# A decoder layer with mixture of experts on one core: the loop over expert passes, run as blocks of eight passes

## The chip, the cores and the metric

The kernel runs on one core of one Trainium2 chip. The metric is the device time of one execution, in microseconds (us). A core has five engines, each with a sequencer of its own that reads its instructions: PE (matrix products), DVE (vector), ACT (scalar), POOL and SP (here it only issues transfers). Loops, branches, register arithmetic and waits are run by the sequencers, and every engine runs its own copy of each loop.

## The reference

One decoder layer on 512 tokens of width 1024, in float32, and a final RMSNorm. Behind the attention part stands the part that fills most of the time, a mixture of 32 experts of which each token uses 4:

```python
def moe(x2d, w_router, b_router, w_in, b_in, w_out, b_out):
    logits = (x2d @ w_router).astype(jnp.float32) + b_router.astype(jnp.float32)
    top_val, top_idx = lax.top_k(logits, TOP_K)
    gates = jax.nn.softmax(top_val, axis=-1)
    ...
    def expert_block(args):
        xb, e = args
        h = xb @ w_in[e] + b_in[e]
        glu = jnp.minimum(h[:, ::2], SWIGLU_LIMIT)
        lin = jnp.clip(h[:, 1::2], -SWIGLU_LIMIT, SWIGLU_LIMIT)
        act = glu * jax.nn.sigmoid(SWIGLU_ALPHA * glu) * (lin + 1.0)
        return act @ w_out[e] + b_out[e]
    ...
    return jax.ops.segment_sum(y, tok_s, num_segments=N)
```

## The kernel before

**Passes.** The tokens of each expert are served in passes of at most 128 (SLOTS). How many passes there are is known only once the router has run: an expert with up to 128 tokens takes one. The bound is MAX_PASSES = 512 * 4 / 128 + 31 = 47; with these inputs there are 33. DVE works out two small tables, `pass_expert` (the expert of each pass) and `pass_first` (its first slot), by way of `pass_diag` and one matmul, each of MAX_PASSES + 1 columns.

**The loop.** Pass 0 is written out. `by_pass` (L441 to L445) then runs passes 1 and up on each engine: a loop over p from 1 to MAX_PASSES - 1 (L443), in which a test (L444) jumps over the body where p isn't below the number of passes. The loop has no early exit, so it counts on to its end. Behind it, `after_last` (L454) reads the number of the last pass from memory, and the rest of the work is written out.

**A pass.** Its weights come as 12 chunks of 1 MB, loaded by SP (`load`, L481) into a ring of 6 slots; a slot is free when ACT and DVE have both read its last chunk. ACT rounds each chunk (`make_hi`, L1084) and DVE takes the rest (`make_lo`, L1514), so that PE can form float32 products from three passes over the chunk (L839, L841, L847). A chunk is 12 matmuls. Four chunks make the first half of the up product of pass p, four the down product of pass p - 1, four the second half of the up product of p. Between them PE makes a list of tokens (L806) and transposes (L814, L865); ACT takes the sigmoid (L1099), DVE makes the rest of SwiGLU (L1526, L1527, L1530); `act_hi` (L1104) and `act_lo` (L1535) split the transposed result. ACT scales the down product's rows (`scale_rows`, L1110). POOL prepares the next list (`prepare_list`, L1706 to L1711), for which DVE's `slots_one_hot` (L1498) waits, gathers the next tokens' rows (L1725) and scatters the result (L1732).

**Behind the loop** comes the down product of the last pass: four chunks, on PE

```python
            done = after_last(pe)
            pe.wait_ge(down_banks_free, done)
            down(done, 0, 0)
            act_transposes(done - 1, 1)
            down(done, 1, 1)
            pe.wait_ge(actT_lo_made, done * 2)
            down(done, 2, 2)
            down(done, 3, 3)
```

SP loads these chunks and then the four parts of the scattered results (parts 0 to 2 at L535, 2 MB each, part 3 in four pieces at L538). The load of part 0 waits until ACT and DVE have read the last chunk of the loop, that of part 1 for two more chunks, that of part 2 for all; part 3 also for the last scatter. DVE's order is: chunks 0 and 1 (`make_lo`), SwiGLU, chunk 2, additions 0 and 1 of part 0 (L1608), `act_lo`, addition 2, chunk 3, addition 3, and then the four additions of each of parts 1, 2 and 3. The final norm and the stores follow.

Of the kernel before, what the change touches and what calls it, by code (L numbers as in the profile page):

```python
# [28 lines left out]
BF16 = mybir.dt.bfloat16  # L29
I32 = mybir.dt.int32  # L30
U32 = mybir.dt.uint32
ALU = mybir.AluOpType
# [17 lines left out]
NE = 32  # L50
# [15 lines left out]
PARTS = 3  # L66
SLOTS = P
MAX_PASSES = SEQ * TOPK // SLOTS + NE - 1
STEPS_PER_PASS = 4
STEPS_TO_ROUTE = 5  # L70
ACT_LIMIT = LIMIT / (1.0 + math.exp(-SWI_ALPHA * LIMIT))
# [11 lines left out]
C_IDENT, C_DECAY, C_QDEC, C_KDEC, C_FREQ = 0, 128, 640, 896, 900  # L83
# [24 lines left out]
def build(nc, x, positions, norm1_g, w_in, lambda_q1, lambda_k1, lambda_q2, lambda_k2, diff_norm_g,  # L108
# [3 lines left out]
    with ctx:  # L112
        def sb(name, shape, dt=F32):
            return ctx.enter_context(nc.sbuf_tensor(name, shape, dt))

        def sem(name):
            return ctx.enter_context(nc.semaphore(name))
# [23 lines left out]
        cst = sb("cst", [P, C_N])  # L141
# [5 lines left out]
        ones_bf = sb("ones_bf", [P, P], BF16)  # L147
# [9 lines left out]
        row_bias = sb("row_bias", [P, 2, 2])  # L157
        row_sum = sb("row_sum", [P, 2, 2])
        row_rec = sb("row_rec", [P, 2, 2])
        pass_expert = sb("pass_expert", [1, MAX_PASSES + 1], I32)  # L160
        passes_upto = sb("passes_upto", [1, NE], I32)
        last_pass = sb("last_pass", [1, 1], I32)
        pos_cur = sb("pos_cur", [P, NT])
# [17 lines left out]
        def w(a, n, rows=P):  # L181
            return work[0:rows, a:a + n]
# [29 lines left out]

        route = w(18944, NT * NE * 4).rearrange("p (i e c) -> p i e c", i=NT, e=NE)
        slot_of = w(19456, NT * NE).rearrange("p (i e) -> p i e", i=NT)
        pass_first = w(19584, MAX_PASSES + 1)
        cum_passes = w(19680, NE)
        n_passes = w(19712, NE)
        expert_count = w(19744, NE)
        scatters_upto = w(19824, NE, 1).bitcast(I32)
        earlier = w(7680, NE)  # L220
        pass_col = w(7712, 4)
        pass_diag = w(7744, MAX_PASSES + 1).bitcast(BF16).rearrange("p (a n) -> p a n", a=2)
        logits = w(20096, NE)
        top8 = w(20128, 8)
        top8_f = w(20136, 8)
# [39 lines left out]
        bank = [pair[i // 2][:, i % 2, :] for i in range(8)]  # L265
# [86 lines left out]
        table_ready = sem("table_ready")  # L352
# [87 lines left out]

        def by_pass(eng, body):  # L441

            with eng.Fori(1, MAX_PASSES) as p:  # L443
                with eng.If(p < passes[eng]):  # L444
                    body(p)  # L445

        passes = {}

        def load_pass_count(eng):
            eng.wait_ge(table_ready, 2)  # L450
            passes[eng] = eng.value_load(at(passes_upto, NE - 1), min_val=1, max_val=MAX_PASSES)

        def after_last(eng):
            return eng.value_load(last_pass[0:1, 0:1], min_val=0, max_val=MAX_PASSES - 1) + 1  # L454

# [92 lines left out]
        def _(pe):  # L548
# [261 lines left out]
            def x_transposes(p, a):  # L810
                if a == 0:
                    pe.wait_ge(gathered, 16 * (p + 1))
                for k in range(KH):
# [4 lines left out]
            gate_transpose(2)  # L818
            gate_transpose(3)
            pe.wait_ge(diag_ready, 1)  # L820
            pe.matmul(bank[7][:, 128:128 + 2 * (MAX_PASSES + 1)], ones_bf[:, :],
                      pass_diag.rearrange("p a n -> p (a n)"), start=True, stop=True).then_inc(pass_rows, 1)
            bias_product(2)
            token_list(0)
# [341 lines left out]
        def _(dve):  # L1166
            chain = Chain(dve, dve_step)
# [295 lines left out]
            for n in range(SLOTS, SEQ, SLOTS):  # L1463
# [16 lines left out]
            chain(dve.tensor_tensor(pass_col[:, 2:3], pass_number, pass_col[:, 1:2], ALU.subtract))  # L1480
            chain.settle()

            near = cst[:, C_IDENT:C_IDENT + MAX_PASSES + 1]
            chain(dve.tensor_scalar(pass_diag[:, 0, :], near, pass_col[:, 0:1], None, ALU.mult))
            dve.tensor_scalar(pass_diag[:, 1, :], near, pass_col[:, 2:3], None, ALU.mult).then_inc(diag_ready, 1)
            dve.wait_ge(pass_rows, 1)
            chain(dve.tensor_scalar(pass_first, bank[7][:, 128 + MAX_PASSES + 1:128 + 2 * (MAX_PASSES + 1)],
                                    float(SLOTS), None, ALU.mult))

            dve.tensor_scalar(pass_expert[:, :], bank[7][0:1, 128:128 + MAX_PASSES + 1], float(NE - 1), None, ALU.min).then_inc(table_ready, 1)  # L1490
            dve.wait_ge(table_ready, 2)
            chain.settle()

# [95 lines left out]
            def counted_pass(p):  # L1589
                chain.before = start + (p - 1) * STEPS_PER_PASS  # L1590
                one_pass(p)
                assert chain.n == STEPS_PER_PASS, chain.n

            by_pass(dve, counted_pass)
            done = after_last(dve)
            chain.before, chain.n = start + (done - 1) * STEPS_PER_PASS, 0
            make_lo(done, 0)
# [24 lines left out]
            chain = Chain(dve, tail_step)  # L1622
# [181 lines left out]
```

## Time and profile before

| what | value |
|---|---|
| time, median of 3 runs | 1616.66 us (1616.61 to 1617.23) |
| span of the profiled execution | 1615.8 us |
| PE busy | 1528.0 us, 95% |
| DVE busy | 1323.2 us, 82% |
| ACT busy | 1007.7 us, 62% |
| POOL busy | 320.3 us, 20% |
| moved by DMA | 476.46 MB |
| span of the loop's passes | about 390 to 1570 us |

The span runs from the first to the last instruction of the one execution that was profiled. It has no other time of its own; the median of the runs is 0.9 us above it. Times in rows are from the span's start. Busy time counts what an engine works, not the register, branch and wait instructions of its sequencer; those appear only where a source line is asked for, under the engine's name with a q (PE's under PEld). The granted clock is given as a share of 2.4 GHz.

### The profile page before, as it was taken

What the parts mean: (1) busy time and instruction counts of PE and PEld (TensorE: products, weight loads), DVE (VectorE), ACT (ScalarE), POOL (GpSimd) and SP (SyncE); (2) the same over time, 40 slices, a digit from 0 to 9 for tenths busy, and PEclk for the clock granted to TensorE, in tenths of its full rate; (3) what the DMA queues carried; (4) which work ended last, traced back from release to release, by engine and by line L of the source; (5) the groups of instructions that cost most, each with busy time, mean ns of one, the idle gap of its engine ahead of it and who ended that gap; (6) DMA issues with size and microseconds to landing.
All of it is one profiled execution on the core that took longest, in us unless ns stands there. A gap on an engine that the chain in (4) does not pass through costs nothing.

```text
span 1615.8 us, 23914 instructions
## 1 busy us (share of the span) xinstructions
PE 1528.0 (95%) x7535; PEld 1253.7 (78%) x7535; DVE 1323.2 (82%) x1276; ACT 1007.7 (62%) x898; POOL 320.3 (20%) x382
## 2 busy tenths in 40 slices
PE   5999679979999999999999999999999999999983
PEld 5999458747888888888888888888888888888872
DVE  3732771368999999998999999999999999999977
ACT  5221551225777777777777777777777777777762
POOL 1000301001222222222222222222222222221210
PEclk9999799859999999999999999999999999999996
DMA  9300701018999999999999999999999999999995
GB/s 266 105 27 1 260 1 46 27 39 294 341 362 366 357 367 364 367 364 368 372 350 361 362 363 369 370 357 376 359 375 347 359 362 366 365 369 363 366 338 222
DMA packets 140909, 476.46 MB, mean 295 GB/s; under 512 B 12160, under 2 KB 28816, under 8 KB 140816
## 3 DMA queue, kind: packets, MB, share of 16 engines
q1 hardware_dynamic: 128096, 445.17, 73.5%
q0 software_dynamic: 10496, 28.74, 5.4%
q10 hardware_dynamic: 2288, 2.17, 0.4%
q8 instruction: 18, 0.29, 0.1%
q14 instruction: 11, 0.09, 0.0%
HBM read 463.45 MB, written 21.50 MB: 300 GB/s over the span
## 4 chain that ended last, share of the span: by engine, by line
PE 90%; DVE 3%; DMA 2%; issue 2%; ACT 2%; ACTq 0%; SPq 0%; DVEq 0%; POOLq 0%
PE pair L839 23%; PE pair L847 23%; PE pair L841 23%; PE pair L727 4%; PE pair L583 3%; PE pair L588 3%; PE pair L584 3%; PE pair L854 2%; PE pair L865 2%; PE pair L814 2%; DMA ring<-in_w_in 1%; PE pair L806 1%; PE pair L776 1%; DMA work<-h_rows,token_next 1%; DVE row_max L1259 1%
## 5 line engine op out<-in xcount | busy, mean ns | idle before, releaser
L1514 DVE TENSOR_TENSOR split<-ring,split 128x2048 fp32r<-128x2048 f32 x396 | 895.7, 2289 | 62.6 <-ACT split L1084 61.5
L1084 ACT CAST split<-ring 128x2048 fp32r<-128x2048 f32 x396 | 756.9, 1912 | 241.3 <-PE pair L847 229.3
L839 PE MATMUL pair<-split,operands 128*128 128x512 f32 x1584 | 639.1, 403 | 8.4 <-issue 7.7
L841 PE MATMUL pair<-split,operands 128*128 128x512 f32 x1584 | 627.1, 396 | 0.0
L847 PE MATMUL pair<-split,operands 128*128 128x512 f32 x1584 | 435.6, 396 | 0.0
L839 PEld LDWEIGHTS pair<-split,operands 128*128 128x128 f32 x1584 | 299.0, 189 | 75.5 <-issue 8.1
L847 PEld LDWEIGHTS pair<-split,operands 128*128 128x128 f32 x1584 | 298.5, 188 | 72.8
L841 PEld LDWEIGHTS pair<-split,operands 128*128 128x128 f32 x1584 | 299.1, 189 | 66.7
L1732 POOL DMA_INDIRECT expert_rows<-work,dest_cur x33 | 68.6, 2080 | 390.0 <-PE pair L847 366.8
L1725 POOL DMA_INDIRECT work<-h_rows,token_next x34 | 76.4, 2248 | 301.7 <-DVE token_next L1509 301.7
L583 PE MATMUL pair<-split,operands 128*128 128x256 f32 x352 | 86.6, 285 | 1.0 <-DVE work L1245 1.0
L1090 ACT CAST operands<-pair 128x512 fp32r<-128x512 f32 x66 | 38.8, 587 | 76.1 <-PE pair L847 42.3
L584 PE MATMUL pair<-split,operands 128*128 128x256 f32 x352 | 86.2, 279 | 0.0
L1706 POOL COPY first_cur<-work 128x1 f32 (+1 forms) x34 | 69.8, 2053 | 41.2 <-issue 32.7
L1738 POOL CAST dest_cur<-list_mid 128x1 int32<-128x1 f32 x33 | 33.1, 1003 | 216.9 <-DMA expert_rows<-work,dest_cur 216.9
L1245 DVE TENSOR_SCALAR work<-pair,stat 128x256 f32<-128x256 f32 x24 | 11.6, 483 | 68.3 <-PE pair L588 68.3
L583 PEld LDWEIGHTS pair<-split,operands 128*128 128x128 f32 x352 | 66.0, 187 | 1.2 <-DVE work L1245 1.2
L584 PEld LDWEIGHTS pair<-split,operands 128*128 128x128 f32 x352 | 66.6, 189 | 0.0
L727 PE MATMUL pair<-late_ring,work 128*128 128x256 f32 x256 | 62.3, 409 | 1.7 <-issue 0.8
L1104 ACT CAST operands<-pair 128x512 fp32r<-128x512 f32 x66 | 38.5, 584 | 36.5 <-PE pair L865 36.5
L727 PEld LDWEIGHTS pair<-late_ring,work 128*128 128x128 f32 x256 | 52.8, 208 | 10.7 <-ACT work L1040 1.2
L978 ACT ACTIVATE work<-pair,stat 128x256 f32<-128x256 f32 x24 | 11.4, 475 | 79.7 <-PE pair L588 75.6
(223 smaller groups left out, 1320.0 us busy)
## 6 DMA issues: line engine op xcount, KB each, us to landing
ring<-in_w_moe_in SPq DMA_DIRECT2D x264, 1024.0 KB, 7.5
ring<-in_w_moe_out SPq DMA_DIRECT2D x132, 1024.0 KB, 9.0
ring<-in_w_in SPq DMA_DIRECT2D x12, 1024.0 KB, 9.5
ring<-expert_rows SPq DMA_DIRECT2D x3, 2048.0 KB, 8.7
late_ring<-in_w_o SPq DMA_DIRECT2D x4, 1024.0 KB, 9.7
resid<-in_x SPq DMA_DIRECT2D x4, 512.0 KB, 7.0
h_rows<-work ACTq DMA_DIRECT2D x4, 512.0 KB, 2.6
late_ring<-expert_rows SPq DMA_DIRECT2D x4, 512.0 KB, 5.8
```

The lines of the kernel that those rows point to most:

```text
L583: pe.matmul(dst, hT_hi[:, k, at_i], w_hi[s][:, k, :], start=(k == 0), stop=False)
L584: pe.matmul(dst, hT_lo[:, k, at_i], w_hi[s][:, k, :], start=False, stop=False)
L588: mm = pe.matmul(dst, hT_hi[:, k, at_i], w_lo[s][:, k, :], start=False, stop=(k == KT - 1))
L727: mm = pe.matmul(dst, mixT[:, i % 2, k, :], slot(s)[:, k, :], start=(k == 0), stop=(k == KT - 1))
L839: pe.matmul(dst[:, f, :], left_hi[:, k0 + k, :], hi[c.buffer][:, k, cols], start=(start and k == 0), stop=False)
L841: pe.matmul(dst[:, f, :], left_lo[:, k0 + k, :], hi[c.buffer][:, k, cols], start=False, stop=False)
L847: mm = pe.matmul(dst[:, f, :], left_hi[:, k0 + k, :], lo[c.buffer][:, k, cols], start=False, stop=(stop and k == 1))
L1084: act.copy(hi[c.buffer], raw[c.slot]).then_inc(hi_made, 1)
L1514: dve.tensor_tensor(lo[c.buffer], raw[c.slot], hi[c.buffer].bitcast(F32), ALU.subtract).then_inc(lo_made, 1)
L1706: chain(pool.tensor_copy(first_cur[:, :], col(pass_first, p)))
L1725: pool.indirect_dma_start(out=x_rows, out_offset=None, in_=h2_dram, in_offset=bass.IndirectOffsetOnAxis(ap=token_next[:, 0:1], axis=0))\
L1732: pool.indirect_dma_start(out=y_dram, in_=y_rows, in_offset=None, out_offset=bass.IndirectOffsetOnAxis(ap=dest_cur[:, 0:1], axis=0), bound ...
```

## The change

`by_pass` becomes two loops. The outer one counts six blocks (BLOCKS), and a test jumps over a whole block if its first pass isn't below the number of passes. The inner one runs the eight passes of a block (IN_BLOCK), each behind the same test as before. The numbers of passes tried go up to 48, so the tables get 50 columns in place of 48 (IN_TABLE). All five engines use `by_pass`.

```diff
+IN_BLOCK = 8
+BLOCKS = (MAX_PASSES - 1 + IN_BLOCK - 1) // IN_BLOCK
+IN_TABLE = BLOCKS * IN_BLOCK + 2
...
         def by_pass(eng, body):
 
-            with eng.Fori(1, MAX_PASSES) as p:
-                with eng.If(p < passes[eng]):
-                    body(p)
+            with eng.Fori(0, BLOCKS) as b:
+                first = eng.snap(b * IN_BLOCK + 1)
+                with eng.If(first < passes[eng]):
+                    with eng.Fori(0, IN_BLOCK) as n:
+                        p = eng.snap(first + n)
+                        with eng.If(p < passes[eng]):
+                            body(p)
...
-        pass_expert = sb("pass_expert", [1, MAX_PASSES + 1], I32)
+        pass_expert = sb("pass_expert", [1, IN_TABLE], I32)
...
-            pe.matmul(bank[7][:, 128:128 + 2 * (MAX_PASSES + 1)], ones_bf[:, :],
+            pe.matmul(bank[7][:, 128:128 + 2 * (IN_TABLE)], ones_bf[:, :],
                       pass_diag.rearrange("p a n -> p (a n)"), start=True, stop=True).then_inc(pass_rows, 1)
```

The other lines of the diff put IN_TABLE for MAX_PASSES + 1 in `pass_first`, `pass_diag` and the four operations of DVE that make the tables.

## Rows read from the trace of the kernel before

**Rows 1.** The page: the span, and one queue of instruction packets.

```profile
span 1615.8 us, 23914 instructions
...
q8 instruction: 18, 0.29, 0.1%
```

**Rows 2.** Windows: length; busy PE, PEld, DVE, ACT, POOL; clock, DMA share, GB/s.

```profile
1200.00:1560.00 360.00, 360.00 (x1645) 292.01 (x1644) 333.44 (x256) 263.48 (x186) 83.56 (x98) 1.00 0.95 360
...
1570.00:1578.00 8.00, 0.32 (x3) 0.04 (x1) 6.04 (x5) 4.09 (x4) 0.49 (x3) 0.66 0.85 337
1578.00:1592.00 14.00, 14.00 (x52) 10.93 (x52) 12.49 (x11) 2.39 (x2) 0.00 (x0) 0.83 0.53 197
```

**Rows 3.** Source view of L444 behind the last pass: duration ns, first and last start.

```profile
L444 SPq COMPARE_BRANCH  x14: 50/50/55, 1549.8 to 1556.3; - x14
...
L444 ACTq COMPARE_BRANCH  x14: 50/50/50, 1561.4 to 1567.1; - x14
...
L444 DVEq COMPARE_BRANCH  x14: 63/63/63, 1563.8 to 1570.7; - x14
...
L444 PEldq COMPARE_BRANCH  x14: 214/214/214, 1566.9 to 1576.6; - x14
```

**Rows 4.** Timeline from the last pass to the end: start, us, what [idle before].

```profile
1549.31 2.28 DVE L1514 TENSOR_TENSOR split<-ring,split 128x2048 fp32r<-128x2048 f32 x1
...
1553.51 8.89 DVE L1514 TENSOR_TENSOR split<-ring,split 128x2048 fp32r<-128x2048 f32 x4
...
1558.12 2.67 SPq L481 DMA_DIRECT2D ring<-in_w_moe_out  x4
...
1563.47 2.29 DVE L1514 TENSOR_TENSOR split<-ring,split 128x2048 fp32r<-128x2048 f32 x1 [0.47 <-ACT split L1084]
...
1568.10 3.71 ACT L1084 CAST split<-ring 128x2048 fp32r<-128x2048 f32 x2 [4.67 <-issue]
...
1577.97 0.79 PE L839 MATMUL pair<-split,operands 128*128 128x512 f32 x1 [7.68 <-issue]
...
1583.07 0.60 PE L865 MATMUL pair<-cst,work 128*128 128x128 f32 x4
...
1584.33 0.69 DVE L1535 TENSOR_TENSOR operands<-pair,operands 128x512 fp32r<-128x512 f32 x1 [1.51 <-ACT operands L1104]
...
1586.13 2.29 DVE L1514 TENSOR_TENSOR split<-ring,split 128x2048 fp32r<-128x2048 f32 x1
...
1590.98 1.10 PE L847 MATMUL pair<-split,operands 128*128 128x512 f32 x4
...
1597.32 4.63 DVE L1608 TENSOR_TENSOR resid<-resid,ring 128x1024 f32<-128x1024 f32 x4 [3.22 <-issue]
...
1602.28 4.87 DVE L1608 TENSOR_TENSOR resid<-resid,late_ring 128x1024 f32<-128x1024 f32 x4 [0.33 <-DMA late_ring<-expert_rows]
```

**Rows 5.** Source view of L535, loads of parts 0 to 2.

```profile
L535 SPq DMA_DIRECT2D ring<-expert_rows x3: 360/365/375, 1565.9 to 1588.5; - x3
...
DMA to landing us min/median/max: 8.2/8.7/11.6
```

**Rows 6.** Groups by line from 430 to 1560: busy us, mean ns | idle before.

```profile
L1084 ACT CAST split<-ring 128x2048 fp32r<-128x2048 f32 x370 | 707.6, 1912 | 214.2 <-PE pair L847 214.2
...
L1498 DVE TENSOR_TENSOR operands<-work,slot_from 128x512 fp32r<-128x512 f32 x31 | 21.5, 693 | 26.1 <-POOL slot_from L1711 26.1
```

**Rows 7.** Timeline of one pass: DVE's subtraction and two copies of POOL.

```profile
1536.01 2.29 DVE L1514 TENSOR_TENSOR split<-ring,split 128x2048 fp32r<-128x2048 f32 x1 [0.82 <-ACT split L1084]
1536.26 2.09 POOL L1706 COPY first_cur<-work 128x1 f32 x1 [1.03 <-issue]
1538.29 0.19 POOL L1707 CAST operands<-work 128x16 fp32r x1
```

**Rows 8.** Queues from 430 to 1560, the first and last listed: packets, MB, share.

```profile
q1 hardware_dynamic: 99923, 385.20, 90.1%
q0 software_dynamic: 8784, 23.91, 5.9%
```

More of the change, by code:

```diff
@@ L214, in build @@
         slot_of = w(19456, NT * NE).rearrange("p (i e) -> p i e", i=NT)
-        pass_first = w(19584, MAX_PASSES + 1)
+        pass_first = w(19584, IN_TABLE)
         cum_passes = w(19680, NE)
@@ L221, in build @@
         pass_col = w(7712, 4)
-        pass_diag = w(7744, MAX_PASSES + 1).bitcast(BF16).rearrange("p (a n) -> p a n", a=2)
+        pass_diag = w(7744, IN_TABLE).bitcast(BF16).rearrange("p (a n) -> p a n", a=2)
         logits = w(20096, NE)
@@ L1481, in _ @@
             chain.settle()
-            near = cst[:, C_IDENT:C_IDENT + MAX_PASSES + 1]
+            near = cst[:, C_IDENT:C_IDENT + IN_TABLE]
             chain(dve.tensor_scalar(pass_diag[:, 0, :], near, pass_col[:, 0:1], None, ALU.mult))
@@ L1486, in _ @@
             dve.wait_ge(pass_rows, 1)
-            chain(dve.tensor_scalar(pass_first, bank[7][:, 128 + MAX_PASSES + 1:128 + 2 * (MAX_PASSES + 1)],
+            chain(dve.tensor_scalar(pass_first, bank[7][:, 128 + IN_TABLE:128 + 2 * (IN_TABLE)],
                                     float(SLOTS), None, ALU.mult))
-            dve.tensor_scalar(pass_expert[:, :], bank[7][0:1, 128:128 + MAX_PASSES + 1], float(NE - 1), None, ALU.min).then_inc(table_ready, 1)
+            dve.tensor_scalar(pass_expert[:, :], bank[7][0:1, 128:128 + IN_TABLE], float(NE - 1), None, ALU.min).then_inc(table_ready, 1)
             dve.wait_ge(table_ready, 2)
```

## Prediction

> **What bounds the kernel now.** I read the page first. The span is 1615.8 us [rows 1]. Cut into stretches, PE is busy for all 360.00 us of 1200 to 1560, at full clock [rows 2]. A pass takes about 36.6 us (370 conversions, 12 to a pass, in the 1130 us of [rows 6]), and that is PE's own work. So nothing inside a pass is worth anything unless it makes PE wait; a gain must come from outside the passes. The same view shows one hole: of the 8 us from 1570 to 1578, PE works 0.32 us, and the granted clock falls to 0.66 of full there and 0.83 in the next stretch [rows 2]. The timeline puts "issue" on that hole [rows 4]: PE waits for no semaphore, its sequencer is busy.
>
> With what, the source view of the loop's test (L444) shows. MAX_PASSES is 47, 33 passes exist (the page has 33 scatters), so the loop runs p = 1 to 32 and then tests 33 to 46 in vain. From the first to the last of these 14 tests it takes 5.7 us on ACT, 6.9 on DVE, 9.7 on PE, 6.5 on SP [rows 3]. One empty iteration (add, back edge taken, move, test jumped) is a thirteenth: **ACT 0.44, DVE 0.53, PE 0.75, SP 0.50 us**. All 14 cost 6.2, 7.4, 10.4 and 7.0 us. Each sequencer reaches the loop's end half an iteration ahead of its first empty test: SP 1549.5, ACT 1561.1, DVE 1563.5, PE 1566.5.
>
> The timeline shows whom that holds up [rows 4]. SP could issue the first load behind the loop when DVE frees its ring slot, at 1549.31 + 2.28 = 1551.6; it issues at 1558.12. ACT starts on it at 1568.10, idle 4.67 us on "issue". PE starts at 1577.97, idle 7.68 us, and runs the first product in 5.10 us (to 1583.07). The 36 matmuls and 4 transposes behind it take 9.01 us (to 1590.98 + 1.10 = 1592.08), so a product at full clock takes 2.9 us at most: the fallen clock costs 2.2 us more.
>
> **The change part by part.**
>
> *The empty tests.* 32 passes are exactly four blocks of eight. Behind the last pass every engine ends the inner loop, takes the outer back edge, tests block 4 (first pass 33, not below 33), tests block 5, and leaves. I put that at three old iterations, one of them for the two loops' ends and the multiply-adds. PE: 2.2 us in place of 10.4, 8.2 saved; ACT 1.3, 4.9 saved; DVE 1.6, 5.8 saved; SP 1.5, 5.5 saved. Bounds: 2 iterations (12 saved) and 5 (9 saved).
>
> On this one price the Trainium skill stands against the rows. Advanced Engine Details and Errata, section Control Flow Timing, gives about 108 ns for a compare-and-branch, so two of them, 0.22 us, for an empty iteration, an estimate from that page; twelve would then save 2.6 us. The rows show two to three times that price on every engine.
>
> *What then limits the tail.* SP needs 1.5 us for the exit and some 1.3 for the reads behind it (now 1556.3 to 1558.12, less the loop's end [rows 3, 4]): it is ready at 1552.3 and issues the four loads as DVE frees slots: 1552.3, 1555.8, 1558.0, 1560.3 (the row at 1553.51, four subtractions in 8.89 us, in bodies that don't move [rows 4]). ACT is ready at 1561.1 + 1.3 + 0.8 = 1563.2; the conversions then wait for PE's products, as in the passes [rows 6], and I take PE's cadence of 2.8 us and 0.4 for transposes: first 1563.9 to 1565.8, second 1567.1 to 1569.0. DVE is ready at 1563.5 + 1.6 + 0.8 = 1565.9, its engine being busy to 1565.76 [rows 4]: subtractions 1565.9 to 1568.2 and 1569.1 to 1571.4, then SwiGLU, three operations on tiles like act_lo's, which takes 0.69 us [rows 4], to 1573.5. PE's sequencer is through at 1568.7 and, with 1.0 us for the read of last_pass and the first wait, ready at 1569.7. Its last matmul of the body ends at 1570.3 (1577.97 - 7.68). **The hole closes whole**, and the clock has nothing to fall for.
>
> Down product 0: 1570.3 to 1573.1. The transposes wait for SwiGLU: 1573.6 to 1573.95. Product 1: to 1576.8. Product 2 waits for act_lo, which on DVE stands behind two additions of part 0: third subtraction 1573.5 to 1575.8, additions to 1578.1 (2.3 us for two), act_lo to 1578.8. Is part 0 there? It is issued at 1565.9 on a release that doesn't move, and landed 11.6 us later, the longest of three [rows 5], because the four late loads were ahead of it. With those out by about 1567.5 it needs some 5 us: 1573, in time. Product 2: 1578.9 to 1581.7, product 3 to 1584.7. Against 1592.08 now: **7.4 us earlier**.
>
> Behind PE come the scaling, the last scatter and the loads of part 3, unchanged: the first addition of part 3, now at 1602.28 [rows 4], could start at 1594.9. But a second route is late next. Part 2 is loaded once the last subtraction is done: act_lo's start + 4.1 (now 1584.33 to 1586.13 + 2.29) = 1582.2. Landing takes 8.2 to 8.7 [rows 5]: 1590.4 to 1590.9 (1597.32 now), and its four additions take 4.63 us [rows 4]: to 1595.5. DVE can't begin on part 3 before, so that addition moves from 1602.28 to 1595.5. **Gain of the tail: 6.8 us.** What follows is a fixed chain.
>
> *What is added to the passes.* A register add in each pass (0.1 us), and between two blocks the inner loop's end, the outer back edge, a multiply-add, a test and two moves: 0.6 to 0.8 us by the rates above, three times, plus about 0.3 once at the entry. What covers it at a pass's end [rows 3, 4]: PE's sequencer is at its loop end 3.8 us before its last matmul ends (1566.5 against 1570.3), DVE's 2.2 us before its engine is free (1563.5 against 1565.76). ACT's engine has a 1.9 us conversion in hand and then idles for PE [rows 6]. SP is 2.1 us ahead of DVE's release and its table reads take most of that, so up to 0.3 us may show there at three borders, for loads that land before they are needed. Cost 0. Without cover it would be 32 x 0.1 + 3 x 0.7 + 0.3 = 5.6 us.
>
> POOL has no such lead: behind its loop end it prepares the list for which DVE idles in every pass, 26.1 us in 31 [rows 6]. One microsecond there would seem to be one on DVE, with the SwiGLU behind it and PE's transposes behind that. But the timeline of one pass [rows 7] has POOL's copy of one column begin 0.25 us after DVE's subtraction and end with it (1536.26 + 2.09 = 1538.35 against 1536.01 + 2.29 = 1538.30), while the copy of sixteen columns behind it takes 0.19. It is held up until DVE is done, whenever it starts. A start 0.1 or 0.6 us later is inside these 2 us. Cost 0; from 2 us on it would be the whole excess.
>
> *The tables.* Two more columns in four small operations on DVE and four in one matmul: under 0.05 us.
>
> Sum on the profiled execution: 1615.8 - 6.8 + 0.1 for leaks = 1609.1. The median of the runs, 1616.66, is 0.9 us above that span, so **1610.0 us**, 0.41% faster.
>
> **The rivals.**
>
> *The clock falls in the small pauses* that remain (0.5 us before the transposes, 2.1 us before product 2). For: it fell inside the pause of 7.68 us [rows 2]. Against: the pauses left are short. One product at 1.2 GHz takes 2.2 us longer; PE then ends at 1586.9, the first addition of part 3 starts at 1597.1, gain 5.2, 1611.5 us. Two products: 1613.7.
>
> *The borders of the blocks show after all*, at PE, by way of POOL or SP: 3 x 0.7 us and part of the 3.2: gain less by 2 to 5, 1612 to 1615. Against it stand the covers above.
>
> *Data hold the tail instead*: part 0 lands as late as now (1577.5), or part 2 needs its 11.6 us. The first puts the additions 1.7 us later, the second part 2 2.9 us: 1611.7 to 1612.9.
>
> *Slower: instruction fetch.* A loop of more blocks and jumps may no longer fit into an engine's instruction memory, and then each pass fetches. The page has instruction packets (18 of 16 KB in one queue [rows 1]), yet from 430 to 1560 the list of queues holds none [rows 8]: today every body stays in. If one engine fell out, a fetch is a DMA and would take between one packet (q8's share in [rows 1] makes about 1.4 us each) and a whole landing (8.2 [rows 5]); I take 3. DVE's cover is 2.2 less some 0.6 for its own loop end, so 1.4 us would show in each of 32 passes: 45 - 7 = 38 us slower, 1655 us. It decides from 0.2 us uncovered per pass. The code grows by some ten instructions an engine, which speaks against it. Runtime: NRT & Kernel Launch of the Trainium skill, section Instruction fetch mechanics, says that a taken branch whose target lies outside a two-page window has to wait for a fetch; no row of this trace shows such a wait.
>
> **How the numbers follow.** As forecast (gain 5.3 to 8): 0.68. Clock: 0.10. Borders: 0.08. Data: 0.06. Fetch: 0.08. The range 1608.2 to 1613.2 takes in the first whole, most of the clock and data cases and the near end of the borders. A measurement of this kernel tells 0.2% (3.2 us, to 1613.4) from nothing. Faster 0.87; within 0.2%, the far ends of clock and borders, 0.05; slower 0.08.
>
> **What would show it.** In the profile after: two empty tests of a block behind the last pass and no more, and a loop exit of about 2.2 us on PE; SP's first load behind the loop near 1552 and the others apart at DVE's pace; PE's idle before the first down product from 7.7 to under 0.5 us, with the clock at full; about 2 us of idle before the third; part 2's first addition near 1591; part 3's near 1595.5; PE without a gap in the passes, also at the three borders. I am wrong if a pass is longer, if instruction packets appear among the passes, or if another wait fills the hole.

## The result, and the profile after

The changed kernel takes 1595.54 us (median of 4 runs, 1592.04 to 1596.2) against 1616.95 us (4 runs, 1616.61 to 1619.96) for the kernel before in the same comparison: a ratio of 0.9862, 95% interval 0.9844 to 0.988. That is 1.4% faster, and 14 us faster than forecast. The profiled execution took 1596.2 us, its span is 1594.4. Of all executions of the study one, of the kernel called e10 below, took 3851.64 us, 2.4 times as long as its three others, and is left out of e10's median.

Behind the loop's code the line numbers of the changed kernel are seven higher than before (L839 is L846, L1514 is L1521). Of the loop itself, L446 is the outer loop, L448 the test of a block, L449 the inner loop and L451 the test of a pass.

First the page of the changed kernel, the two lines that answer to [rows 1].

```profile
span 1594.4 us, 23774 instructions
...
q8 instruction: 18, 0.29, 0.1%
```

The span is 21.4 us shorter. The instruction packets are as many as before, 18 in q8, and the queues of the stretch of the passes again list none.

```profile
q1 hardware_dynamic: 101496, 391.37, 91.4%
q0 software_dynamic: 8928, 24.17, 5.9%
```

So no instruction packet falls into the passes, but q1 moved 391.37 MB in the 1130 us for which [rows 8] has 385.20. The passes themselves run faster, which no step of the prediction had. The windows of the changed kernel (length; busy PE, PEld, DVE, ACT, POOL with counts; granted clock, DMA share, GB/s) say the same:

```profile
1200.00:1560.00 360.00, 359.62 (x1667) 294.15 (x1666) 337.62 (x258) 265.06 (x189) 102.77 (x96) 1.00 0.97 368
1554.00:1562.00 8.00, 7.62 (x35) 5.74 (x33) 7.60 (x7) 5.06 (x5) 1.79 (x3) 1.00 1.01 386
1562.00:1577.00 15.00, 5.83 (x25) 4.43 (x24) 12.06 (x11) 2.69 (x3) 1.86 (x1) 0.92 0.57 215
```

PE is as busy as before over the 360 us, at the same granted clock of 1.00 (2.4 GHz), yet it has 1667 matmuls there and not 1645 [rows 2]. A share of busy time can't show that: the matmuls follow each other faster. The second window holds the place where the hole was: PE works 7.62 of 8 us, and the clock stays at 1.00. In the third it stays at 1.00 up to 1569.5, where PE's last matmul ends, and is lower only behind that.

The pass's list of tokens is a good clock, since every pass makes one (four matmuls, L806 before, L813 after). These are the source views of the kernel before and of the changed one: duration, first and last start.

```profile
L806 PE MATMUL pair<-operands x136: 165/251/372, 355.2 to 1542.9; 128*128 128x4 f32 x136
```

```profile
L813 PE MATMUL pair<-operands x136: 167/251/373, 353.6 to 1528.4; 128*128 128x4 f32 x136
```

They cut the profiled executions into three parts. (The last list begins 0.3 us before the start of its fourth matmul, which the rows give.)

| part, us | before | after | difference |
|---|---|---|---|
| start to the first list | 355.19 | 353.61 | -1.58 |
| first to last list | 1187.42 | 1174.50 | **-12.92** |
| last list to the end (the tail) | 73.18 | 66.32 | **-6.86** |

The first part is the same work in both; it took 348.6 to 356.8 us in the profiled executions of this study, in no order that follows the edits. The third is what the prediction was about: 6.8 us forecast, 6.86 measured. The second is the surprise: a steady pass took 36.733 us before and 36.318 after, so 31 of them give 12.9 us.

Here is the tail of the changed kernel in the timeline, lines that answer to [rows 4]:

```profile
1538.03 8.42 SPq L488 DMA_DIRECT2D ring<-in_w_moe_out  x4
...
1549.17 1.92 ACT L1091 CAST split<-ring 128x2048 fp32r<-128x2048 f32 x1 [0.36 <-PE pair L854]
...
1551.36 2.29 DVE L1521 TENSOR_TENSOR split<-ring,split 128x2048 fp32r<-128x2048 f32 x1 [0.23 <-ACT split L1091]
...
1555.35 0.39 PE L846 MATMUL pair<-split,operands 128*128 128x512 f32 x1
...
1558.64 0.66 PE L872 MATMUL pair<-cst,work 128*128 128x128 f32 x4 [0.38 <-DVE work L1537]
...
1563.80 0.49 PE L846 MATMUL pair<-split,operands 128*128 128x512 f32 x1 [1.74 <-DVE operands L1542]
...
1568.49 1.07 PE L854 MATMUL pair<-split,operands 128*128 128x512 f32 x4
...
1575.61 4.63 DVE L1615 TENSOR_TENSOR resid<-resid,ring 128x1024 f32<-128x1024 f32 x4 [2.94 <-issue]
1580.16 1.22 DVE L1615 TENSOR_TENSOR resid<-resid,late_ring 128x1024 f32<-128x1024 f32 x1
1582.02 3.77 DVE L1615 TENSOR_TENSOR resid<-resid,late_ring 128x1024 f32<-128x1024 f32 x3 [0.64 <-DMA late_ring<-expert_rows]
```

The idle of 7.68 us ahead of the first down product is gone: the row at 1555.35 has no bracket. The reader is to compare the brackets that are left. PE waits 0.38 us for SwiGLU and 1.74 us for act_lo, and for nothing else; DVE waits 2.94 us for part 2. The loop's exit on PE in the source views of the test of a block, the inner loop's end behind the last pass and the read of last_pass (duration; first and last start):

```profile
L448 PEldq COMPARE_BRANCH  x6: 73/83/216, 389.9 to 1553.2; - x6
...
L449 PEldq COMPARE_BRANCH  x1: 67/67/67, 1551.8 to 1551.8; - x1
...
L461 PEldq TENSOR_LOAD <-last_pass x1: 324/324/324, 1553.7 to 1553.7; - x1
```

Six tests of a block in the whole program, two of them behind the last pass (1552.5 and 1553.2), and from the inner loop's end to the read of last_pass 1.9 us, where 2.2 were forecast and the kernel before took 10.4. And the landings of parts 0 to 2, which answer to [rows 5]:

```profile
DMA to landing us min/median/max: 8.0/9.3/10.1
```

### The profile page after: what moved, and what is told of

It is laid out like the page before. It is cut to its first block, busy times and chain, and to the rows that moved or that the text cites. A ratio compares the mean times of both kernels' runs of the same rounds, so it can differ in the third digit from the quotient of the medians.

```text
span 1594.4 us, 23774 instructions
## 1 busy us (share of the span) xinstructions
PE 1509.3 (95%) x7535; PEld 1247.3 (78%) x7535; DVE 1321.7 (83%) x1276; ACT 1008.6 (63%) x898; POOL 374.8 (24%) x382
## 4 chain that ended last, share of the span: by engine, by line
PE 90%; DVE 3%; DMA 2%; ACT 2%; issue 2%; SPq 0%; DVEq 0%; POOLq 0%; ACTq 0%
PE pair L846 23%; PE pair L854 23%; PE pair L848 22%; PE pair L734 4%; PE pair L590 3%; PE pair L591 3%; PE pair L595 3%; PE pair L861 2%; PE pair L821 2%; PE pair L872 2%; DMA ring<-in_w_in 1%; PE pair L813 1%; PE pair L783 1%; DMA work<-h_rows,token_next 1%; DVE row_max L1266 1%
## 5 line engine op out<-in xcount | busy, mean ns | idle before, releaser
L1521 DVE TENSOR_TENSOR split<-ring,split 128x2048 fp32r<-128x2048 f32 x396 | 895.1, 2288 | 45.0 <-ACT split L1091 44.9
L1091 ACT CAST split<-ring 128x2048 fp32r<-128x2048 f32 x396 | 757.6, 1914 | 228.9 <-PE pair L854 221.7
L846 PE MATMUL pair<-split,operands 128*128 128x512 f32 x1584 | 633.7, 400 | 2.6 <-DVE operands L1542 1.7
L854 PE MATMUL pair<-split,operands 128*128 128x512 f32 x1584 | 432.0, 395 | 0.0
L854 PEld LDWEIGHTS pair<-split,operands 128*128 128x128 f32 x1584 | 295.6, 188 | 73.1 <-DVE split L1521 9.4
L846 PEld LDWEIGHTS pair<-split,operands 128*128 128x128 f32 x1584 | 298.5, 188 | 64.1 <-issue 2.2
L1739 POOL DMA_INDIRECT expert_rows<-work,dest_cur x33 | 77.9, 2360 | 372.9 <-PE pair L854 358.3
L1097 ACT CAST operands<-pair 128x512 fp32r<-128x512 f32 x66 | 38.8, 587 | 73.1 <-PE pair L854 40.9
L1713 POOL COPY first_cur<-work 128x1 f32 (+1 forms) x34 | 64.9, 1908 | 42.8 <-issue 34.3
L1725 POOL CAST operands<-work 64x128 fp32r x34 | 73.8, 2170 | 1.0 <-PE pair L854 1.0
L734 PEld LDWEIGHTS pair<-late_ring,work 128*128 128x128 f32 x256 | 53.3, 210 | 10.8 <-issue 1.2
L1745 POOL CAST dest_cur<-list_mid 128x1 int32<-128x1 f32 x33 | 20.7, 626 | 157.8 <-DMA expert_rows<-work,dest_cur 157.8
```

The costliest lines, as they stand in the source:

```text
L734: mm = pe.matmul(dst, mixT[:, i % 2, k, :], slot(s)[:, k, :], start=(k == 0), stop=(k == KT - 1))
L846: pe.matmul(dst[:, f, :], left_hi[:, k0 + k, :], hi[c.buffer][:, k, cols], start=(start and k == 0), stop=False)
L854: mm = pe.matmul(dst[:, f, :], left_hi[:, k0 + k, :], lo[c.buffer][:, k, cols], start=False, stop=(stop and k == 1))
L1091: act.copy(hi[c.buffer], raw[c.slot]).then_inc(hi_made, 1)
L1521: dve.tensor_tensor(lo[c.buffer], raw[c.slot], hi[c.buffer].bitcast(F32), ALU.subtract).then_inc(lo_made, 1)
L1713: chain(pool.tensor_copy(first_cur[:, :], col(pass_first, p)))
```

## The experiments

Two questions are open: what made the passes faster, and whether the tail went by the steps of the prediction or only by their sum. The tails that the expectations below quote are counted 10.5 to 10.9 us longer than those of this text (76.9 there is 66.3 here), because their end was counted from a zero that lies that far ahead of the first instruction; differences between them aren't touched by it.

The wider table explains more than its four instructions. pass_expert grew from 192 to 200 bytes in each partition. In the compiled kernels these tiles begin at multiples of 32 bytes, so every tile behind it moved by 32. The chunks' ring, their split copies and the residual rows lie ahead of it and stay. The large area `operands`, which holds the left sides of the products (what PE loads as weights), begins at byte 142368 before and at byte 142400 after. 142368 is 32 past a multiple of 64; 142400 is a multiple of 64. So two things changed at once, the loop and the place. An unused small tile behind the table moves the place alone.

### The loop and the place, apart

e1 is the changed kernel moved by 32 bytes more (142432); e2 is the kernel before moved to the changed kernel's place (142400); e3 is the kernel before at e1's place (142432).

```diff
         pass_expert = sb("pass_expert", [1, IN_TABLE], I32)
+        sb("spacer", [1, 8], I32)
```

(e2 the same behind the kernel before's table, e3 with 16 columns.)

> The changed kernel with an unused tile of 32 bytes behind the table, so that the operand tile starts 32 bytes past a multiple of 64, as in the kernel before (there it starts at byte 142368, in the changed kernel at 142400, here at 142432). Theory A (the passes got faster because the wider table moved the tiles that PE loads as weights from 32 past a multiple of 64 onto one): a pass takes 36.73 us again, and what is left of the gain is the tail alone, 6.8 us: 1610 us. Theory B (the new loop's code itself makes PE's matmuls closer): still 36.3 us a pass, 1595 to 1596 us.

> The kernel before, its loop and its table of 48 columns unchanged, with an unused tile of 32 bytes behind the table, so that the operand tile starts at byte 142400, as in the changed kernel. Theory A: 36.3 us a pass, the tail as before: 1616.9 less 31 x 0.41 and 1.6 ahead of the passes = 1602.6 us. Theory B: 1617 us.

> The kernel before with an unused tile of 64 bytes behind the table: the operand tile starts at byte 142432, again 32 past a multiple of 64, with exactly the addresses of the first kernel of this batch. Theory A: no change, 1617 us, so that the two differ by the loop alone, 6.8 us. If any shift of the addresses counts and not the place within 64 bytes, it leaves 1617 us.

Windows from 430 to 1500 of the changed kernel, then of e1, e2 and e3. The first pair is busy PE and its matmuls.

```profile
430.00:1500.00 1070.00, 1070.00 (x4951) 875.93 (x4950) 1000.24 (x769) 792.94 (x561) 309.67 (x298) 1.00 0.97 367
```

```profile
430.00:1500.00 1070.00, 1070.00 (x4909) 869.01 (x4907) 993.48 (x758) 785.82 (x556) 254.33 (x294) 1.00 0.97 365
```

```profile
430.00:1500.00 1070.00, 1070.00 (x4953) 876.54 (x4952) 1001.24 (x771) 792.46 (x560) 310.47 (x295) 1.00 0.97 367
```

```profile
430.00:1500.00 1070.00, 1070.00 (x4911) 869.23 (x4910) 993.36 (x760) 784.15 (x555) 254.62 (x293) 1.00 0.97 364
```

A pass has 168 matmuls, so 4951 in 1070 us are 36.31 us a pass, and 4911 are 36.60. Both loops at 142400 make 4951 and 4953; both loops at 142432 make 4909 and 4911. The loop has no part in it.

| kernel | loop | `operands` at | median us (range) | ratio to before [95%] | first to last list | pass | tail |
|---|---|---|---|---|---|---|---|
| before | old | 142368 | 1616.95 | 1 | 1187.42 | 36.733 | 73.18 |
| e3 | old | 142432 | 1610.88 (1607.79 to 1614.71) | 0.9967 [0.9952, 0.9981] | 1184.69 | 36.633 | 72.96 |
| e1 | new | 142432 | 1605.1 (1602.03 to 1608.97) | 0.9919 [0.9893, 0.9944] | 1184.41 | 36.633 | 66.03 |
| e2 | old | 142400 | 1599.42 (1597.17 to 1606.37) | 0.9903 [0.9868, 0.9938] | 1173.94 | 36.300 | 72.60 |
| after | new | 142400 | 1595.54 (1592.04 to 1596.2) | 0.9862 [0.9844, 0.988] | 1174.50 | 36.318 | 66.32 |

The last three columns are of the profiled executions, one for each kernel. From e3 to e1, the same place, the loop is worth 6.93 us of tail and nothing in the passes; from e2 to after 6.28 us. The place is worth 10.8 us in the passes with the old loop (e3 to e2) and 9.9 with the new one (e1 to after), and nothing in the tail beyond its scatter: 72.6 to 74.1 us in the four kernels with the old loop, 65.7 to 67.6 in the eight with a new one and this order of the tail. The two causes add. By the medians, which scatter more, the loop is worth 5.8 and 3.9 us and the place 11.5 and 9.6.

Not all of it came as expected. e3 was to stay at 1617 us and took 1610.88: its pass is 0.10 us shorter than the kernel before's, 2.7 us in all, and its profiled execution was 6.6 us earlier at the first list. e1, at the same place, was to have a pass of 36.73 us and 1610 us, and has 36.633 and 1605.1. e2's median lies 3.2 us under the 1602.6 expected. So 142368 and 142432, both 32 past a multiple of 64, aren't equal.

### Which tile it is

The spacer moves more than the left sides: the small tiles behind it, the bias rows in `operands`, and the work area, which begins at the same byte, with the rows that are transposed. e4 is the changed kernel in which only the left sides inside `operands` stand 32 bytes later; e10 is the kernel before with the same edit, which puts them, and nothing else, on a multiple of 64. In e5 the changed kernel's stand 16 bytes later.

```diff
-            return operands[:, a:a + KT * SLOTS].rearrange("p (k t) -> p k t", k=KT)
+            return operands[:, a + 8:a + 8 + KT * SLOTS].rearrange("p (k t) -> p k t", k=KT)
...
-        b_in_parts = operands[:, 4096:4096 + 2 * FF]
+        b_in_parts = operands[:, 4112:4112 + 2 * FF]
...
-        pick_bias = operands[:, 6144:6144 + SLOTS]
+        pick_bias = operands[:, 6160:6160 + SLOTS]
```

(In e5 the 8 is a 4. The bias rows and the row that picks them move by 64 bytes to make room, in all three.)

> The changed kernel, in which only the four stationary operands of the passes (the split tokens and the split activations) are moved by 8 elements, 32 bytes, within the operand tile; the bias rows and the selection row behind them move by 64 bytes to make room. All else, the part ahead of the passes too, stays on multiples of 64. Theory A, in its narrow form (it is the weight loads): 36.73 us a pass and the part ahead of the passes fast, 1595.5 + 31 x 0.41 = 1608.2 us. If it is something else that moved with the tile (the rows that are transposed, the additions, the loads from the ring): 1595.5 us.

> The kernel before, with its loop, its table and all its tiles where they are; only the four stationary operands of the passes are moved by 8 elements within the operand tile, so that they start on a multiple of 64 bytes (the bias rows and the selection row move by 64 bytes). Theory A (the place of the weight loads within 64 bytes sets the pace of the matmuls): 36.3 us a pass in place of 36.73, the part ahead of the passes as before, 1617 - 31 x 0.42 = 1604 us. If the passes of the changed kernel were faster because of the other tiles that moved: 1617 us.

> The changed kernel with the same four stationary operands moved by 4 elements, 16 bytes, off the multiple of 64. If what counts is how many stretches of 64 bytes a row of 512 bytes touches (8 when it starts on a multiple, else 9), a shift of 16 is as bad as one of 32: about 36.7 us a pass, 1608 us. If only the halves of 64 bytes count (a read of 32 bytes on its own boundary or not), 16 is worse than 32: over 36.8 us a pass. If 16 bytes are the grain: 36.3 us, 1595.5 us.

The same window of e4 and of e10:

```profile
430.00:1500.00 1070.00, 1070.00 (x4899) 867.91 (x4898) 990.27 (x759) 784.55 (x555) 254.67 (x294) 1.00 0.97 364
```

```profile
430.00:1500.00 1070.00, 1070.00 (x4951) 876.14 (x4950) 999.97 (x768) 792.33 (x561) 317.23 (x298) 1.00 0.97 367
```

e4 loses nearly all that the passes had won (median 1608.25, 0.9946 [0.9929, 0.9962], pass 36.694), and e10 wins all of it with the old loop and the old table (median 1605.4, 0.9931 [0.9903, 0.9958], pass 36.323). It is the place of the left sides. e5 lies between: 1602.81 us, 0.9915 [0.9894, 0.9936], pass 36.607; its 16 bytes cost 0.29 us a pass where e4's 32 cost 0.38. That is none of the three outcomes that were written down for e5, so none of the three rules behind them is borne out.

e12 asks whether 142400 was only a lucky address. It is the changed kernel with a spacer of 16 columns, `operands` at 142464, the next multiple of 64.

> The changed kernel with an unused tile of 64 bytes behind the table, so that the area of the left operands stands at 142464, the next multiple of 64 (the changed kernel: 142400; 32 bytes off: 142432). Theory (what counts is the place of the left operand within 64 bytes): matmul steps 229.1 ns, passes 36.32 us, as in the changed kernel. Rival (the one address, not its remainder, was lucky, or any unused tile makes the passes slower): steps near 233 ns, passes 36.6 us or more.

It took 1597.98 us (1595.61 to 1601.45), 0.9881 [0.9856, 0.9907]; pass 36.294 us, so the rival falls. But the step from one matmul to the next, start to start, wasn't the 229.1 ns expected. 142464 is also a multiple of 128, and there the step is shorter still and varies by 1 ns. The steps of the pass's 128x512 products, read from the starts of the matmuls in the traces, in order and as two means: over 46 steps in the first half of the up product, in 31 passes, and over all steps under 245 ns of these passes:

| left sides begin at | past a multiple of 128 | kernels | steps in their order, ns | mean, first half | mean, all |
|---|---|---|---|---|---|
| 142464 | 0 | e12 | 227, 227, 226, ... | 226.7 | 227.8 |
| 142400 | 64 | after, e2, e10 | 226, 229, 232, ... | 228.9 | 229.2 to 229.4 |
| 142416 | 80 | e5 | 227, 231, 236, 233, 229, 233, 235, 228, 234, ... | 231.7 | 232.5 |
| 142432 | 96 | e1, e3; e4 | 231, 235, 233, 234, ... | 233.3 to 233.4 | 232.8; 233.2 |
| 142368 | 32 | before | 237, 231, 232, ... | 233.4 | 233.3 |

The order isn't kept everywhere: in e12 steps of 228 to 236 ns follow a wait before it settles, and in e5's last chunks it is 233, 233, 234. The place on 128 was tried in one kernel.

Why, then, is e12's pass only 0.02 us shorter than the changed kernel's? Weight loads of L854 (L855 in e1 and e12) from 430 to 1500: busy us, mean ns, idle before and who ended it; the changed kernel, e1, e12.

```profile
L854 PEld LDWEIGHTS pair<-split,operands 128*128 128x128 f32 x1415 | 263.4, 188 | 65.4 <-DVE split L1521 8.8
```

```profile
L855 PEld LDWEIGHTS pair<-split,operands 128*128 128x128 f32 x1400 | 262.4, 187 | 64.3
```

```profile
L855 PEld LDWEIGHTS pair<-split,operands 128*128 128x128 f32 x1416 | 263.5, 188 | 68.9 <-DVE split L1522 14.5
```

A wait for DVE's remainder appears that the slower kernel doesn't have, 8.8 us in some 29 passes, and grows to 14.5 where PE is faster still. In a pass of the changed kernel the 57th and 58th of the large matmuls start on average 264 and 337 ns after the one ahead (232 and 237 before), in e12 458 and 333. PE has caught up with DVE there, and e12's 0.19 us more of waiting eats nearly all that its shorter steps win. What then holds a pass at 36.3 us isn't one busy engine: in e12, from 430 to 1500, DVE works 1001.06 us of 1070.00 and itself waits 33.2 us for ACT's conversions and 25.2 for GpSimd's list. That chain wasn't taken apart.

### The loop's form

e8 has no empty tests at all, a loop over the counted passes. e6 has blocks of four, e7 of sixteen.

```diff
-            with eng.Fori(0, BLOCKS) as b:
-                first = eng.snap(b * IN_BLOCK + 1)
-                with eng.If(first < passes[eng]):
-                    with eng.Fori(0, IN_BLOCK) as n:
-                        p = eng.snap(first + n)
-                        with eng.If(p < passes[eng]):
-                            body(p)
+            with eng.Fori(1, passes[eng]) as p:
+                body(p)
```

```diff
-IN_BLOCK = 8
+IN_BLOCK = 4
```

(e7: 16.) The table keeps its 50 columns in all three, and so the place stays.

> The changed kernel's tables and addresses, but one loop on each engine from 1 up to the number of passes itself, held in a register: no test, no empty pass. Theory of the tail (PE's sequencer was through 3 us before its last matmul ended, so what the two tests left cost nothing): the tail from the last list of tokens to the end stays at 76.9 us, and the time at 1595.5 us. If every empty test still shows: 2 x 0.75 us less, 1594 us. If the inner test and add cost in the passes, 0.1 us in each: 3 us less.

> The changed kernel with blocks of four: 7 borders between blocks among the 32 passes in place of 3, and four more empty outer tests behind the last pass (blocks 8 to 11 and the loop's end in place of 4 and 5, but no more table use). The table stays 50 columns wide, so the tiles stand where they stand in the changed kernel. Theory of the prediction (borders are covered by every engine's lead at a pass's end, and an empty outer test costs about 0.75 us on PE, with PE's first down product not waiting for the exit by some margin): passes 36.32 us with no border visible, the exit on PE 1.5 us longer, and PE idle before the first down product grows from none to at most 1.5 us; tail 76.9 to 78.4 us. Rival (a border costs 0.7 us uncovered): 4 x 0.7 = 2.8 us more from the first list to the last.

> The changed kernel with blocks of sixteen: one border among the passes in place of three, and one empty outer test behind the last pass in place of two. Theory: passes 36.32 us, nothing gained at borders; SP's and PE's exit 0.5 to 0.75 us shorter, behind which PE wasn't waiting anyway: tail 76.4 to 76.9 us, median within 1 us of the changed kernel's 1595.5. Rival (borders cost 0.7 us each): 1.4 us less from the first list to the last.

| kernel | borders in the passes | empty outer tests behind | median us | ratio [95%] | first to last list | tail |
|---|---|---|---|---|---|---|
| e8 | none | none | 1596.82 | 0.9872 [0.9855, 0.9888] | 1174.21 | 66.43 |
| e7 | 1 | 1 | 1594.8 | 0.9845 [0.9817, 0.9874] | 1174.44 | 66.80 |
| after | 3 | 2 | 1595.54 | 0.9862 [0.9844, 0.988] | 1174.50 | 66.32 |
| e6 | 7 | 4 | 1592.31 | 0.984 [0.9819, 0.9861] | 1174.61 | 66.54 |

Four loops, one time: the lengths agree to 0.5 us. Borders and the tests that are left cost nothing that can be seen. e8, with neither, has the changed kernel's tail to 0.1 us. That fits the leads of the sequencers that the prediction counted, and e6 shows where PE's ends. Its outer tests behind the last pass, and its first down product:

```profile
L448 PEldq COMPARE_BRANCH  x4: 214/214/216, 1553.0 to 1555.2; - x4
```

```profile
1556.67 0.49 PE L846 MATMUL pair<-split,operands 128*128 128x512 f32 x1 [0.60 <-issue]
```

Three intervals in 2.2 us are 0.73 us for one empty outer test on PE, the price that the prediction took from [rows 3] (0.75). Two tests more than the changed kernel's make 1.5 us, 0.9 of it is under cover and 0.60 shows; the tail is 0.2 us longer.

### The order of the tail

The forecast had PE wait 2.1 us for act_lo behind two additions (1.74 measured). e9 lets DVE do act_lo and the last subtraction first, and only then the additions.

```diff
-            add_part(0, 0)
-            add_part(0, 1)
             act_lo(done - 1, 1)
-            add_part(0, 2)
             make_lo(done, 3)
-            add_part(0, 3)
+            for i in range(NT):
+                add_part(0, i)
```

> The changed kernel with DVE's order behind the loop altered: the split of the transposed result and the fourth subtraction come ahead of the four additions of part 0. If the pause of PE ahead of the third down product (1.74 us in the profile of the changed kernel) is due to the two additions, it closes: PE ends 1.7 us earlier, part 2 is loaded 2.8 us earlier, and the end comes 1.7 us earlier, 1593.8 us. If something else is just behind (ACT's conversion, the landing of part 2): less than 0.5 us.

It missed: 1601.56 us (1600.23 to 1603.9), 0.9904 [0.9888, 0.9921], the tail 70.68 us and so 4.4 longer. PE did lose its pause: its third down product has no bracket, and its last matmul ends at 1567.17, 2.4 us earlier.

```profile
1561.51 0.39 PE L846 MATMUL pair<-split,operands 128*128 128x512 f32 x1
```

The timelines of e9's DVE and GpSimd:

```profile
1563.59 13.71 DVE L1615 TENSOR_TENSOR resid<-resid,ring 128x1024 f32<-128x1024 f32 x12
1584.46 2.48 DVE L1615 TENSOR_TENSOR resid<-resid,late_ring 128x1024 f32<-128x1024 f32 x2 [7.16 <-DMA late_ring<-expert_rows]
...
1569.29 8.87 POOL L1737 DMA_INDIRECT expert_rows<-work,dest_cur  x1 [12.55 <-ACT work L1117]
```

and of the changed kernel's GpSimd:

```profile
1571.69 1.86 POOL L1739 DMA_INDIRECT expert_rows<-work,dest_cur  x1 [14.56 <-ACT work L1117]
```

The last scatter began 2.4 us earlier and ended 4.6 us later: GpSimd worked 8.87 us on it (times on GpSimd are rough), until 0.9 us behind DVE's last addition (1577.3). SP, which waits for the scattered rows to land, issues part 3 at 1580.46 where the changed kernel has 1575.84, and DVE waits 7.16 us for part 3. In the changed kernel DVE happened to stand still from 1572.67 to 1575.61, and the scatter fell into that gap. The wait for rows_sent that DVE has between parts 1 and 2 doesn't hold it: GpSimd's sequencer raises that semaphore as it passes, 0.2 us before the scatter's own instruction begins, and not when GpSimd is done with the scatter.

That is a theory with a test. e11 is e9 with the semaphore raised by a small GpSimd operation behind the scatter, and DVE's wait ahead of the sixth addition.

```diff
-            for i in range(NT):
-                add_part(1, i)
+            add_part(1, 0)
             dve.wait_ge(rows_sent, 1)
+            for i in range(1, NT):
+                add_part(1, i)
...
-            pool.sem_inc(rows_sent, 1)
+            pool.memset(pass_number, 0.0).then_inc(rows_sent, 1)
```

> As the run with part 0's additions last (e9), but DVE makes only five of its twelve additions before it waits for a small GpSimd operation placed behind the last scatter, so that DVE stands still while GpSimd builds the scatter's descriptors. Theory (DVE's additions, back to back, kept the scatter from being built: 8.87 us in that run against 1.86 in the changed kernel): PE still has no pause before the third down product, the scatter starts near 1569.3 and now takes under 2.5 us, lands 4 to 5 us later, DVE resumes near 1571.5, has seven additions of 1.15 us left to about 1579.5, and part 3 is in by then; the tail from the last token list is 74.8 to 75.8 us against 76.9 in the changed kernel and 81.2 in e9: median 1594 to 1595 against 1595.5. Rival (the scatter was slow because its start met other transfers, or because it begins 2.4 us earlier, whatever DVE does): it takes 5 us or more again and the tail stays above 79 us. Passes 36.32 us in both.

```profile
1560.37 5.76 DVE L1615 TENSOR_TENSOR resid<-resid,ring 128x1024 f32<-128x1024 f32 x5
1567.22 8.04 DVE L1615 TENSOR_TENSOR resid<-resid,ring 128x1024 f32<-128x1024 f32 x7 [1.09 <-POOL work L1786]
1575.17 4.63 DVE L1615 TENSOR_TENSOR resid<-resid,late_ring 128x1024 f32<-128x1024 f32 x4
...
1566.08 1.00 POOL L1738 DMA_INDIRECT expert_rows<-work,dest_cur  x1 [12.56 <-ACT work L1117]
```

DVE gives up 1.09 us, the scatter takes 1.00 and not 8.87, and DVE then has no wait left to the last addition of part 3. The tail is 63.94 us, 2.4 less than the changed kernel's and 6.7 less than e9's, a little better than the theory's window, and under the 65.7 to 67.6 us of all the kernels with the old order. The median is 1589.84 us (1588.42 to 1593.74), 0.9832 [0.9807, 0.9858], the lowest of the study and 4 us under what was expected; of the distance between the two profiled executions the tail accounts for 2.4 us, and 3.8 lie ahead of the passes, where executions differ. The intervals of the two kernels overlap, so that e11 beats the changed kernel rests on the tail, of one trace each. A rule of the Trainium skill stands beside this: GPSIMD Engine Reference, section Key points, says that GpSimd shares its SBUF interfaces with VectorE and contends with instructions that have two SBUF inputs. These additions have two, and the trace agrees. SBUF — State Buffer, section Who interferes with whom, infers that such an addition doesn't hold up the building of descriptors; the 8.87 us against 1.00 speak against that, and the measurement decides.

## Why the prediction was wrong, and where it was right

**The step that failed** is "*The tables.* Two more columns in four small operations on DVE and four in one matmul: under 0.05 us." The working priced the instructions that touch the table and not what its size does to the tiles behind it. What the runs showed in its place: 32 bytes of displacement, which put the left sides on a multiple of 64, take 4 ns off every large matmul, some 0.58 us for the 144 of a pass; about 0.13 us of that goes into the new wait for DVE, and a pass is 0.42 us shorter. With 31 steady passes that is 12.9 of the 14.5 us between forecast and measurement; the other 1.6 lie ahead of the passes, where executions differ. The range fell with it, because nothing in the sum or the rivals could make a pass shorter. That a pass's time is PE's own work was right; it was then taken as a fixed quantity (of about 36.6 us, read from 370 conversions; the lists give 36.733). PE was busy for all 360.00 us and still had 1.1% in hand. The trace had the hint: steps of 231, 232 and 237 ns in turn, in a row of equal matmuls.

**The tail** went as worked out up to PE's end, and its sum is in part luck. Shift the forecast times by 14.50 us, the lead of the changed kernel at its last list:

| step | forecast, shifted | measured |
|---|---|---|
| SP's first load behind the loop | 1537.8 | 1538.03 |
| ACT's first conversion | 1549.4 | 1549.17 |
| DVE's first subtraction | 1551.4 | 1551.36 |
| PE's down product 0 | 1555.8 | 1555.35 |
| product 1 | 1559.4 | 1559.06 |
| product 2, behind act_lo | 1564.4 | 1563.80 |
| PE's last matmul ends | 1570.2 | 1569.56 |
| part 2's first addition | 1576.4 | 1575.61 |
| part 3's first addition | 1581.0 | 1580.16 |

The largest error is 0.8 us. Part of it is the faster product (12 steps of 228.9 ns are 2.75 us, 2.8 was taken). The part 3 additions then wait 0.64 us for a landing. The forecast called what follows a fixed chain and had no such wait; without it the gain would be 7.5 and not 6.86, so two errors of opposite sign make up the 6.8. It was lucky with part 0 as well: it gave part 0 some 7 us from its issue to be in, and part 0 took 9.3 (from 1551.2 to 1560.5), which was still just ahead of its first addition at 1560.71.

**The empty tests** cost what [rows 3] said: 0.73 us on PE in e6, against 0.75. By the Trainium skill's price (Advanced Engine Details and Errata, section Control Flow Timing; 0.22 us for two branches, the prediction's estimate) e6's two tests more would be 0.44 us, inside the 0.9 us of cover, and e6 would have no idle of 0.60 us. The prediction's 2.6 us for that price counts twelve iterations, its bound; the eleven of its own sum make 2.4.

**The covers** held. Three borders, seven, one and none give first-to-last times within 0.4 us of each other. POOL's lead isn't what it was, though. The copy of one column is still held under DVE's subtraction (mean 2032 ns, 2185 before), but another cast (L1725) now takes 2338 ns on average in the changed kernel's passes. In one pass it begins at 1512.62, 0.12 us after a subtraction of 2.29 us; in the kernel before it began 0.18 us ahead of one (1526.55 against 1526.73):

```profile
L1725 POOL CAST operands<-work 64x128 fp32r x31 | 72.5, 2338 | 0.0
```

In the kernel before the same operation (L1718) took 333 ns. POOL had that time to spare: DVE waits 0.84 us a pass for POOL's list in both.

**The rivals.** The clock stayed at 1.00 (2.4 GHz) through the two small pauses (of 0.38 and 1.74 us). Part 2 took 8.5 us from its issue (1567.12) to its first addition, as taken. No instruction packet came up in the passes. The borders stayed hidden. None of the four was the way in which it went; the list lacked "the place of a tile changes the speed of the instruction that reads it".

**Left open.** Why a step depends on the left side's place is not shown, nor whether the place of the other operand matters: the weight load's own mean is 188 ns at 142400 and 187 to 188 at 142432, so it isn't in the load's duration. Nor is it clear why 142368 and 142432, with steps of nearly the same mean, differ by 0.1 us a pass, what holds e12's pass at 36.3 us, or what makes the first 350 us vary by 8.

## What to carry to other kernels

When an edit changes the size of any on-chip tile, write down where the large operands stand before and after, and test the place alone with an unused tile; otherwise what the place does is put down to the edit. In a stretch in which PE is always busy, divide the window's length by its matmuls and compare with the best step seen for that shape: that is the share that "busy" hides. And when DVE's work behind a loop is packed closer, look at what GpSimd has to issue there; here a wait of 1.09 us, ended by an operation behind the scatter and not by the sequencer, made the tail 6.7 us shorter than without it.

## What the hardware showed that was not expected

- A 128x512 product whose left side begins on a multiple of 128 bytes follows the last one after 226.7 ns on average, varying by 1 ns once settled (e12 alone); 64 past it 228.9, 80 past it 231.7, 32 or 96 past it 233.3 to 233.4 ns. All at a granted clock of 1.00.
- The 2% between 228.9 and 233.4 ns never show as idle time: 1070.00 us busy of 1070.00 in the changed kernel and in e1.
- The last scatter kept GpSimd for 8.87 us under back-to-back additions of 128x1024 floats on DVE, 1.86 us with part of it in a gap, 1.00 us while DVE waited.
- A semaphore raised by GpSimd's sequencer behind an indirect transfer rose 0.23 us before the transfer's own instruction began.
